# Conditioning products formed by GpSimd during other stages, in a two-block transformer kernel on one core

## The reference

```python
# first block, each of two layers (c: one row)
mod = silu(c) @ ada_w[layer] + ada_b[layer]          # (1024) x (1024, 6144)
sh1, sc1, g1, sh2, sc2, g2 = split(mod, 6)
# mixer on x * (1 + sc1) + sh1, gated by g1, layer norm;
# feed-forward on x * (1 + sc2) + sh2, gated by g2, layer norm

# second block, each of two layers: one row for x, one for the context
mod_l = silu(c_2) @ w_mod[layer] + b_mod[layer]
mod_c = silu(c_ctx) @ w_mod[layer] + b_mod[layer]
```

## Time and profile before

| | |
|---|---|
| time, median of 3 runs | 4277.1 us (4276.34 to 4279.16) |
| the profiled execution's own time | 4276.59 us |
| its span | 4274.8 us |
| busy in the span | PE 3166.1 us (74%), VectorE 2299.4 (54%), ScalarE 1045.3 (24%), GpSimd 932.1 (22%) |
| HBM read | 1050.12 MB, 246 GB/s over the span |

### The profile page before, as it was taken

The page is one execution under the profiler, slowest core; times in us unless marked ns, Lnnn a source line. Parts: engine busy times, 40 slices in busy tenths (PEclk is TensorE's granted clock), DMA queues, the critical chain, the costliest instruction groups (busy, mean ns, idle before and its releaser), DMA issues. The chain is left out here.

```text
span 4274.8 us, 37661 instructions
## 1 busy us (share of the span) xinstructions
PE 3166.1 (74%) x12012; PEld 1860.5 (44%) x12012; DVE 2299.4 (54%) x4802; ACT 1045.3 (24%) x2385; POOL 932.1 (22%) x804
## 2 busy tenths in 40 slices
PE   5767975977976868798777777777666664777776
PEld 1657933962734746233232232222264563322322
DVE  4456645746156338744665665555433648655554
ACT  1335422531232332111111111111232241111112
POOL 0000000000000012344444444444100023444442
PEclk9868997998986589999999999999987777999999
DMA  7214552536200111999999999999530034999996
GB/s 286 91 40 138 175 223 99 184 131 230 78 0 0 40 54 64 383 415 422 421 421 421 421 422 421 422 421 422 222 130 0 1 114 172 422 421 421 422 421 260
DMA packets 166466, 1052.95 MB, mean 246 GB/s; under 512 B 18332, under 2 KB 22172, under 8 KB 55344
## 3 DMA queue, kind: packets, MB, share of 16 engines
q0 software_dynamic: 110592, 805.36, 45.4%
q1 hardware_dynamic: 55728, 245.89, 16.0%
HBM read 1050.12 MB, written 1.05 MB: 246 GB/s over the span
## 5 line engine op out<-in xcount | busy, mean ns | idle before, releaser
L1800 PE MATMUL peer_fetch_summed<-peer_fetch_raw,peer_fetch_diag 128*128 128x512 f32 x3072 | 1443.4, 616 | 501.7 <-ACT peer_fetch_diag L1739 501.7
L1696 DVE CUSTOM_DVE_ANT_0 peer_fetch_raw<-peer_fetch_raw,peer_rows 128x1024 f32<-128x1024 f32 x768 | 940.2, 1225 | 852.6 <-DMA peer_fetch_raw<-in_peer_uv,peer_fetch_experts 852.1
L1800 PEld LDWEIGHTS peer_fetch_summed<-peer_fetch_raw,peer_fetch_diag 128*128 128x128 f32 x3072 | 567.2, 193 | 1368.7 <-ACT peer_fetch_diag L1739 777.4
L1618 POOL DMA_INDIRECT peer_fetch_raw<-in_peer_uv,peer_fetch_experts x768 | 855.6, 1114 | 1188.8 <-PE peer_fetch_summed L1800 1058.2
L1543 POOL TENSOR_TENSOR peer_keys_lo<-peer_pick_wq_raw,peer_keys_hi 128x1024 fp32r<-128x1024 f32 x32 | 76.3, 2389 | 2096.8 <-ACT peer_keys_hi L1502 2096.8
L1730 ACT ACTIVATE peer_fetch_gelu<-peer_fetch_score 128x2 f32<-128x2 f32 x384 | 78.1, 203 | 1629.2 <-DVE peer_fetch_score L1696 1629.2
L1739 ACT ACTIVATE peer_fetch_diag<-all_constants,peer_fetch_gelu 128x128 f32<-128x128 f32 x768 | 260.1, 386 | 0.5 <-issue 0.2
L124 PE MATMUL ffn_up_acc<-first_h_hi,ffn_up_hi 128*128 128x256 f32 x704 | 201.3, 286 | 36.9 <-DVE ffn_up_lo L644 36.9
L124 PE MATMUL ffn_up_acc<-first_h_lo,ffn_up_hi 128*128 128x256 f32 x704 | 200.9, 285 | 0.0
L124 PE MATMUL ffn_up_acc<-first_h_hi,ffn_up_lo 128*128 128x256 f32 x704 | 200.8, 285 | 0.0
L452 PE MATMUL mod_acc<-mod_weights,mod_act_c 128*1 128x512 f32 (+1 forms) x288 | 135.6, 615 | 43.9 <-DMA mod_weights<-in_ada_w 30.6
(11 more groups left out here) (483 smaller groups left out, 4808.0 us busy)
## 6 DMA issues: line engine op xcount, KB each, us to landing
mod_weights<-in_ada_w SPq DMA_DIRECT2D x48, 1024.0 KB, 7.4
in_up_raw<-in_w_up SPq DMA_DIRECT2D x88, 512.0 KB, 4.1
mod_weights<-in_w_mod SPq DMA_DIRECT2D x24, 1024.0 KB, 5.9
peer_fetch_next_raw<-in_w_mod SPq DMA_DIRECT2D x24, 1024.0 KB, 8.8
ffn_down_raw<-in_w_down SPq DMA_DIRECT2D x32, 704.0 KB, 5.6
peer_pick_wq_raw<-in_peer_wq SPq DMA_DIRECT2D x32, 512.0 KB, 3.3
peer_fetch_raw<-in_peer_uv,peer_fetch_experts POOLq DMA_INDIRECT x768, 19.0
in_in_raw<-in_ab_w_in SPq DMA_DIRECT2D x17, 512.0 KB, 3.4
```

The costliest lines, as they stand in the source:

```text
L1618: nc.gpsimd.indirect_dma_start(raw[:, n % ring].rearrange("p c d -> p (c d)"), None, uv_rows, bass.IndirectOffsetOnAxis(index[:, i, e:e + ...
L1696: nc.vector.tensor_tensor_reduce(raw[:, n % ring, 0, :], raw[:, n % ring, 0, :], rows[:, i, :], 1.0, 0.0, ALU.mult, ALU.add, score[:, i, e ...
L1800: ins = nc.tensor.matmul(summed[:, i % 2, half, :], diag[:, n % dring, :], raw[:, n % ring, 1, half * 512:(half + 1) * 512], start=(e == 0 ...
```

## The change

- `modulation` keeps 4 of mod0's 12 groups (shift and scale of the first mixer) as a stage. mod1 and mod20 are gone as stages. mod0 applies SiLU to both vectors.
- A new class `Quiet` forms the other 32 groups ("tasks") on GpSimd: 8 of mod0 and 12 of mod1 with one column, 12 of mod20 with two. A task has four units; a unit is one DMA of 512 KB that GpSimd itself issues into a ring of two slots, then two multiplications by SiLU's column (L574) and two additions into a row of 128x512 (L578). Each dependent step waits for a semaphore.
- `form(count)` is GpSimd's body in these stages, with so many tasks: ab_in 3, ab_v 1, hgrn_scores 2, swa_attention 2, ab_out 1, ln00 1, ffn0_up 8, ln01 1 (all with one column), pool 2 (one with one column, one with two), ffn1_up 4, ffn1_down 1, mlstm_scan 3, window_attention 3 (with two).
- Later a stage settles the rows: TensorE adds each over partitions in pieces of 128 columns against a column of ones (`collect`, L593), VectorE adds the bias (`settle`). That is in cat_split (2 tasks, 8 matmuls), ln00 (7, 28), ln01 (9, 36), ln10 (3, 16), ln11 (5, 40), rope2 (3, 24) and cat2_split (3, 24).
- In the up stage of `conv_ffn` the buffer `hidden` has 2 slots instead of 22, since the ring and the rows take room.

The diff, cut to its core:

```diff
+class Quiet:
+
+
+    UNITS = 4
+
+    def __init__(self, nc, st, name, ring, rows, tasks, ones):
+        self.nc, self.ring, self.rows, self.tasks, self.ones = nc, ring, rows, tasks, ones
+        self.slots = ring.shape[1]
+        self.s_loaded = [st.sem(f"{name}_loaded{r}") for r in range(self.slots)]
+        self.s_term = st.sem(f"{name}_term")
+        self.term = Steps(nc.gpsimd, self.s_term)
+        self.formed, self.settled, self.row = 0, 0, 0
+        self.place = {}
+
+    def fetch(self, pool, unit):
+        if unit >= self.UNITS * len(self.tasks):
+            return
+        job, g = self.tasks[unit // self.UNITS]
+        quarter = unit % self.UNITS
+        src = job["weights"][2 * g + quarter // 2][:, quarter % 2 * 2:quarter % 2 * 2 + 2]
+        pool.dma_start(self.ring[:, unit % self.slots], src).then_inc(self.s_loaded[unit % self.slots], 16)
+
+    def form(self, pool, count, spare=None):
+
+
+
+        if self.formed == 0:
+            for unit in range(self.slots):
+                self.fetch(pool, unit)
+        for task in range(self.formed, self.formed + count):
+            silu = self.tasks[task][0]["silu"]
+            n = silu.shape[2]
+            self.place[task] = [self.rows[(self.row + j) % len(self.rows)] for j in range(n)]
+            self.row += n
+            for quarter in range(self.UNITS):
+                unit = task * self.UNITS + quarter
+                slot = unit % self.slots
+                pool.wait_ge(self.s_loaded[slot], 16 * (unit // self.slots + 1))
+                for j, mine in enumerate(self.place[task]):
+                    raw = self.ring[:, slot]
+                    scaled = raw if j == n - 1 else spare
+                    for i in range(2):
+                        k = quarter * 2 + i
+                        self.term.done(self.nc.gpsimd.tensor_scalar(mine if k == 0 else scaled[:, i, :], raw[:, i, :],
+                                                                    silu[:, k, j:j + 1], None, ALU.mult))
+                    self.term.wait()
+                    for i in range(1 if quarter == 0 else 0, 2):
+                        self.term.link(self.nc.gpsimd.tensor_tensor(mine, mine, scaled[:, i, :], ALU.add))
+                self.fetch(pool, unit + self.slots)
+        self.formed += count
+
+    def settling(self, last):
+
+        tasks = range(self.settled, last)
+        self.settled = last
+        return tasks
+
+    def collect(self, pe, tasks, acc, s_cols):
+        at = 0
+        for task in tasks:
+            for m in range(4):
+                for mine in self.place[task]:
+                    ins = self.nc.tensor.matmul(acc[:, at:at + 1], mine[:, m * P:(m + 1) * P], self.ones[:, 0:1], start=True, stop=True)
+                    at += 1
+        ins.then_inc(s_cols, 1)
+
+    def settle(self, dve, tasks, acc, s_cols, s_biased):
+        nc = self.nc
+        dve.wait_ge(s_cols, 1)
+        at, count = 0, 0
+        for task in tasks:
+            job, g = self.tasks[task]
+            n = job["silu"].shape[2]
+            mine = slice(4 * g, 4 * g + 4)
+            nc.vector.tensor_tensor(job["mods"][:, mine, :], acc[:, at:at + 4 * n].rearrange("p (m n) -> p m n", n=n),
+                                    bcast(job["bias"][:, mine], n), ALU.add).then_inc(s_biased, 1)
+            at += 4 * n
+            count += 1
+        dve.wait_ge(s_biased, count)
+        for task in tasks:
+            job, g = self.tasks[task]
+            if 4 * g // KD in (1, 4):
+                mine = job["mods"][:, 4 * g:4 * g + 4, :]
+                nc.vector.tensor_scalar(mine, mine, 1.0, None, ALU.add)
 
 
...
-        modulation(nc, "mod0", c, d["ada_w"][0], ada_b(0), mods, con("ident"))
+        c_2 = vec("c_2").rearrange("p (k n) -> p k n", n=2)
+        layers = [{"weights": d["ada_w"][0], "silu": silu[:, :, 0:1], "bias": ada_b(0), "mods": mods[0]},
+                  {"weights": d["ada_w"][1], "silu": silu[:, :, 0:1], "bias": ada_b(1), "mods": mods[1]},
+                  {"weights": d["w_mod"][0], "silu": silu[:, :, 1:3], "bias": vec("b_mod_2")[:, 0:6 * KD], "mods": mods_2}]
+        tasks = [(layers[0], g) for g in range(4, 12)] + [(layers[1], g) for g in range(12)] + [(layers[2], g) for g in range(6)]
+        ring, sums = blk.sb("ring", [P, 2, 2, 512]), blk.sb("sums", [P, 10, 512])
+        spare = h.rearrange("p k t -> p (k t)").rearrange("p (u c) -> p u c", c=512)
+        quiet = Quiet(nc, blk, "quiet", ring, [sums[:, r, :] for r in range(10)], tasks, con("ones"))
+
+        modulation(nc, "mod0", [(silu[:, :, 0:1], c), (silu[:, :, 1:3], c_2)], silu[:, :, 0:1], 4, d["ada_w"][0], ada_b(0),
+                   mods[0], con("ident"))
         with Stage(nc, "in00") as st:
             ahead = Ahead(nc, st, "in", d["ab_w_in"])
-            modulate(nc, "h00", h, pair, x, mods, 0, (0,), ahead)
-            even_mixer(nc, d, ahead, pair, z, mods, vec, con)
-        layer_norm(nc, "ln00", x, z, h, T, *ln(0, 0), con("mean_of_d"))
+            modulate(nc, "h00", h, pair, x, mods[0], 0, (0,), ahead)
+            even_mixer(nc, d, ahead, pair, z, mods[0], vec, con, quiet)
+        layer_norm(nc, "ln00", x, z, h, T, *ln(0, 0), con("mean_of_d"), quiet=(quiet, 1), settle=(quiet, 9))
         with Stage(nc, "in01") as st:
             ahead = Ahead(nc, st, "up", d["w_up"][0])
-            modulate(nc, "h01", h, pair, x, mods, 3 * KD, (0,), ahead)
-            conv_ffn(nc, "ffn0", pair, ahead, conv(0), d["w_down"][0], z, mods[:, 5 * KD:, :])
-        layer_norm(nc, "ln01", x, z, h, T, *ln(0, 1), con("mean_of_d"))
-
-        modulation(nc, "mod1", c, d["ada_w"][1], ada_b(1), mods, con("ident"))
-        modulate(nc, "h10", h, pair, x, mods, 0, (0,))
-        pool_mixer(nc, "pool", h, d["pool_w"], vec("pool_scale"), d["inv_count"], z, mods[:, 2 * KD:3 * KD, :], x)
-        layer_norm(nc, "ln10", x, z, h, T, *ln(1, 0), con("mean_of_d"), residual=False)
+            modulate(nc, "h01", h, pair, x, mods[0], 3 * KD, (0,), ahead)
+            conv_ffn(nc, "ffn0", pair, ahead, conv(0), d["w_down"][0], z, mods[0][:, 5 * KD:, :], (quiet, 8))
+        layer_norm(nc, "ln01", x, z, h, T, *ln(0, 1), con("mean_of_d"), quiet=(quiet, 1), settle=(quiet, 18))
+
+        modulate(nc, "h10", h, pair, x, mods[1], 0, (0,))
+        pool_mixer(nc, "pool", h, d["pool_w"], vec("pool_scale"), d["inv_count"], z, mods[1][:, 2 * KD:3 * KD, :], x,
+                   (quiet, 2, sums[:, 2:4]))
+        layer_norm(nc, "ln10", x, z, h, T, *ln(1, 0), con("mean_of_d"), residual=False,
+                   settle=(quiet, 21))
         with Stage(nc, "in11") as st:
             ahead = Ahead(nc, st, "up", d["w_up"][1])
-            modulate(nc, "h11", h, pair, x, mods, 3 * KD, (0,), ahead)
-            conv_ffn(nc, "ffn1", pair, ahead, conv(1), d["w_down"][1], z, mods[:, 5 * KD:, :])
-        layer_norm(nc, "ln11", x, z, h, T, *ln(1, 1), con("mean_of_d"))
+            modulate(nc, "h11", h, pair, x, mods[1], 3 * KD, (0,), ahead)
+            conv_ffn(nc, "ffn1", pair, ahead, conv(1), d["w_down"][1], z, mods[1][:, 5 * KD:, :],
+                     (quiet, 4, spare), (quiet, 1, spare))
+        layer_norm(nc, "ln11", x, z, h, T, *ln(1, 1), con("mean_of_d"), settle=(quiet, 26))
 
 
...
-            hidden = up.sb("hidden", [P, KF, T])
+            hidden = up.sb("hidden", [P, 2, T])
...
-            token_major(nc, "ab_v", d["ab_w_v"], 5 * P, h, T, v)
+                     (inv_freq[:], d["inv_freq"]), (mask[:], d["swa_mask"])], (quiet, 3))
+            token_major(nc, "ab_v", d["ab_w_v"], 5 * P, h, T, v, (quiet, 1))
...
-            decayed_scores(nc, "hgrn_scores", q[:], k[:], [(g[:], False)], [masks], at[:], [off[:]])
+            decayed_scores(nc, "hgrn_scores", q[:], k[:], [(g[:], False)], [masks], at[:], [off[:]], quiet=(quiet, 2))
...
-            mlstm(nc, "mlstm_scan", q, k, v, rows, u_cols, masks, select, con("ones"), o)
+            quiet.rows = [cat[:, r, :] for r in range(H, KD)] + [h[:, r, :] for r in range(6, KD)]
+            mlstm(nc, "mlstm_scan", q, k, v, rows, u_cols, masks, select, con("ones"), o, (quiet, 3, h[:, 4:6]))
...
-            attention(nc, "window_attention", tiles, vec("sinks_2"), cat[:, H:, :], con("ident"))
+            attention(nc, "window_attention", tiles, vec("sinks_2"), cat[:, H:, :], con("ident"), (quiet, 3, h[:, 4:6]))
```

154 lines of the change are left out of this document (107 added, 47 removed).

## The result

The changed kernel took 4544.9 us (median of 4 runs, 4541.3 to 4548.4), the kernel before, on the same chip, 4276.7. The ratio is 1.064, with a 95% interval of 1.060 to 1.069: **slower by 268 us**, where the prediction said 27 slower and gave 4415 as its upper end. The profiled execution spans 4541.6 us, 266.8 more than before.

What follows compares the result with a forecast made beforehand. The prediction took each barrier-closed stage to last as long as its slowest engine. With 213.3 us removed and 240.5 given back, +27 on 4276.6 gave 4304 us, range 4105 to 4415 for 8 in 10.

Steps and rivals of the forecast that it cites:

- what bounds the kernel: Whole kernel: stages closed by barriers of all engines, so each lasts as long as its slowest engine.
- what is removed: Conditioning stages: mod1 whole (80.4 us), mod20 whole (86.8), eight of mod0's twelve groups (46.1), together 213.3 us.
- What one task costs GpSimd: GpSimd's price per task from its multiplications (0.6 us each), additions (1.2), DMA issues (0.94) and waits.
- T1 in swa_attention outside 16 to 20: Sign of being wrong: a one-column task in swa_attention taking GpSimd less than 16 or more than 20 us.
- T1: GpSimd's time for a task with one column, forecast at 17.5 us.
- T2: GpSimd's time for a task with two columns, forecast at 31.2 us.
- rival 2: GpSimd and VectorE hinder each other, but GpSimd is quick: T1 14.7, T2 27.5, total 4227 us; chance 0.2.
- 0.85 of VectorE's two-input time: Stages with tasks: GpSimd waits during 85% of VectorE's two-input work, as in ffn0_up 68.7 us.
- No row shows VectorE waiting for GpSimd: The trace showed only GpSimd waiting; VectorE's possible 66 us in ffn_up was left out of the sum.
- cover of 20 us: window_attention: its tasks need 94.6 of 115.2 us, so nothing is given back; cover gone at T2 = 38.
- The additions over partitions: TensorE's 176 one-column matmuls, 0.3 us each: ln11 +7 us, rope2 and cat2_split together +5.
- Rival 3: GpSimd is slow, TENSOR_SCALAR 0.9 and TENSOR_TENSOR 1.3 us, or TensorE is starved at a lower clock: 4412 us; chance 0.15.

Runs made afterwards that it cites:

- experiment 1: The changed kernel with GpSimd's arithmetic left out except one multiplication per task and column, the loads kept; 4086.1 us.
- experiment 2: The changed kernel with GpSimd's multiplication as a TENSOR_TENSOR, SiLU's column repeated along the row, instead of TENSOR_SCALAR; 4438.5 us, ratio 1.038.
- experiment 6: The changed kernel with only 16 of the 32 groups hidden, the rest kept as stages, and the multiplication as TENSOR_TENSOR; 4291.1 us, ratio 1.003.
- experiment 8: The kernel before, plus unneeded GpSimd work without loads: 40 TENSOR_TENSOR in ffn0_up, 40 TENSOR_SCALAR in ffn1_up; 4289.1 us.
- experiment 9: The kernel of experiment 6 (16 of 32 groups hidden) with the multiplication as TENSOR_SCALAR again; 4262.2 us, ratio 0.996.
- experiment 11: The changed kernel with only seven of the 32 groups hidden, none in an up stage, and the multiplication as TENSOR_SCALAR; 4243.9 us, ratio 0.994.

## Why the prediction failed

- **The direction, what bounds the kernel and what is removed: right.** Slower was given 0.54, and slower it was, but by ten times the 27 us. Of the stages taken out 213.3 us were forecast, 217 came. The loads cost nothing in the stages they moved to (experiment 1).
- **The step that failed: the price of TENSOR_SCALAR in "What one task costs GpSimd".** It took 0.6 us, near the lower bound, "since it reads one tensor where the other reads two". It takes 1.56, outside the bounds of 0.49 to 1.2: the count of inputs was no guide to its time on GpSimd. One of the prediction's own signs of being wrong, T1 in swa_attention outside 16 to 20, came with 25.6. 8 x 0.96 = 7.7 us on T1, 15.4 on T2. The addition was mis-sized by little (1.27 for 1.2), the DMA issue was right (0.60 and 0.30 of wait, for 0.94). Together T1 is 8.1 and T2 16.6 too low. In stages that GpSimd ended stood 19 tasks of the one kind and 8 of the other, and now the three of window_attention too: 19 x 8.1 + 8 x 16.6 + 28.5 = 315 us.
- The rule of the Trainium skill that rival 2 named (GPSIMD Engine Reference, Engine selection: one-input work roughly at line rate), an estimate of 0.43 us, is 3.6 times too quick here. Its figure for two inputs (Elementwise), from which 1.3 us followed, agrees with the 1.27 measured.
- **The second term that was off: 0.85 of VectorE's two-input time added to GpSimd.** It made 220 us over all stages. Over all of its 352 multiplications and 308 additions GpSimd lost some 110 (1050 us busy for 352 x 1.56 + 308 x 1.27), four fifths of it on the multiplications; in ffn0_up 28 for 68.7. That is 110 less than forecast. So the two errors went opposite ways: +315 - 110 = +205, of the 237 by which what was given back (477) exceeds the forecast (240.5). A third piece that the sum lacked more than covers the other 32: the 3.9 to 5.2 us at the end of the 11 stages that GpSimd ends behind the issue of a load, 46 in all. The two sums above are too rough to close it nearer.
- **"No row shows VectorE waiting for GpSimd": it does, and I had left its price out of the sum.** I noted that by the rule of the Trainium skill (SBUF — State Buffer, Who interferes with whom) VectorE would get longer too, by 66 us in ffn_up, and dismissed it since GpSimd's own end came later. For this kernel that was so: VectorE got 41 us longer in ffn0_up and was still done 67 us before the stage ended. But it decided the stages as soon as GpSimd was quicker or had less to do: experiments 2, 6, 8 and 9 show it with GpSimd off the path. For TENSOR_TENSOR the trace agrees with the rule that one waits for the other's whole instruction; beside a TENSOR_SCALAR VectorE lost little and GpSimd the more (experiment 8).
- **window_attention: wrong as a consequence.** Its cover of 20 us "is gone at T2 = 38"; T2 was 47.8, and it gave back 28.5.
- The additions over partitions were right in kind: ln11 +8.4 for 7, rope2 and cat2_split +8.7 for 5.
- Rival 3 (GpSimd slow, with TENSOR_SCALAR at 0.9) was the nearest case, and still 133 us short. Its other way to the same end, TensorE starved at a lower clock, wasn't what bound this kernel, but came in part in experiment 6 (0.88 in ffn0_up). The range was too narrow since both bounds of an instruction that no row showed were taken from other instructions. For a term that enters 352 times, 0.5 to 1.2 was no bound.

## What to carry to other kernels

Price an instruction on GpSimd only from a row of the same operation on GpSimd; where there is none, measure it alone first, since a term with a count of 352 decides the sign. Count what GpSimd's last issue of a load leaves at a barrier, 4 to 5 us here. Work moved to GpSimd isn't free when it ends before the stage does: look for VectorE instructions with SBUF operands that stand in the chain to TensorE, be they 128x2, and count a whole GpSimd instruction for each that may meet one. Move little, to stages without such a chain, and weigh a slower instruction that lets VectorE through against a quicker one that doesn't.

## What the runs showed of the hardware that was not expected

- GpSimd's TENSOR_SCALAR of 128x512 f32 takes 1.56 us (1.50 with a constant), beside VectorE in ffn0_up 2.00 on the mean (1.61 with a constant), its TENSOR_TENSOR of the same size 1.27, and 1.04 if one operand is a column repeated along the row.
- Beside GpSimd's TENSOR_TENSOR, VectorE's instructions from SBUF wait for its end: a `lo` of 1.22 us takes up to 2.3, a 128x2 of 0.16 takes 0.89 on the mean. Beside TENSOR_SCALAR they go on at about half their rate or better (hidden_lo 0.42 to 0.83), and GpSimd's goes from 1.56 to 2.04 on the mean, up to 2.9. A VectorE product with one operand in PSUM kept its 0.41 beside both.
- VectorE's TENSOR_SCALAR with one tensor as input waits too (L665: 0.41 to 0.64 on the mean, 1.4 at most), with a column or with constants.
- A plain DMA issue blocks GpSimd for 0.60 us, and a stage that GpSimd ends with one goes on for 3.9 to 5.2 us behind it.
- The granted clock of window_attention moved with no edit there: 0.50 before (115.2 us), 0.60 in experiment 8 (103.6), 0.62 in experiment 1 (100.5), 0.55 in experiment 11 (111.1). What set it wasn't tried; a comparison of totals within 15 us should look at this stage first, and at the first peer fetch, which moved by up to 12 us with no edit of its own.
